# Modulation vectors by transposition and a sum on VectorE, and the last four norms in halves of 256 tokens

## The chip, the core and the metric

One core of one Trainium2 chip runs the whole program in one launch. The metric is the device time of one execution in microseconds (us). Engines in the rows: PE is TensorE (PEld its weight loads), DVE is VectorE, ACT is ScalarE, POOL is GpSimd, SP is SyncE, which only issues transfers.

## What is computed

Two blocks over 512 tokens of 1024 features, float32, one after the other. The first (differential attention, a short convolution, an output product, a gate) is not touched except that four modulation vectors are made beside it. The second, cut to what matters:

```python
def rmsnorm(x, g):
    y = xf * lax.rsqrt(jnp.mean(xf * xf, axis=-1, keepdims=True) + EPS)
    return y * g
def modulate(h, shift, scale):
    return h * (1.0 + scale[:, None, :]) + shift[:, None, :]
...
c_act = jax.nn.silu(c)
for i in range(2):
    mod = c_act @ w_ada[i] + b_ada[i]
    sh1, sc1, g1, sh2, sc2, g2 = jnp.split(mod, 6, axis=-1)
    h = modulate(rmsnorm(x, norm_mix_g[i]), sh1, sc1)
    m = fourier_mixer(h, w_fourier_out) if i == 0 else retention_mixer(h, w_ret_in, w_ret_out)
    x = x + g1[:, None, :] * m
    h = modulate(rmsnorm(x, norm_ffn_g[i]), sh2, sc2)
    x = x + g2[:, None, :] * swiglu(h, w_ffn_in[i], w_ffn_out[i])
shf, scf = jnp.split(c_act @ w_ada_final + b_ada_final, 2, axis=-1)
return modulate(rmsnorm(x, final_norm_g), shf, scf)
```

So there are 14 modulation vectors of 1024 numbers, each a vector times a 1024x1024 matrix, and each norm needs, for every token, the sum of squares over all 1024 features before any feature of it can be scaled.

## The kernel before

Tensors lie feature-major: `X[:, m, :]` is feature tile m (128 features on the partitions) by 512 tokens, m from 0 to 7. A product of K input tiles gives output tile m by K steps (k, m), and each step is three matmuls of 128x128 weights by 512 tokens, since every float32 operand is split in a high and a low part of type float32r: low weights by high data (L1361), high by low (L1364), high by high (L1365). `gemm_order` takes output tiles 0 to 3 together with k outermost (the last two k tile by tile), and then tiles 4 to 7 one after the other. Outputs lie in seven PSUM banks by the tables `BANK` and `TURN`; bank 7 is `aux`, for small products.

Weights come as one stream of 259 chunks of eight 128x128 tiles. SP loads a chunk into a ring of four (L295), ACT writes the high part (`split_w`, L379), POOL the low part in four pieces (L355), and PE signals `w_used` when it begins the next chunk. Every engine's order is written out by hand, and engines wait for each other on semaphores; a wait holds everything behind it on that engine.

**Modulation vectors.** SP streams each 1024x1024 matrix in eight row blocks of 512 KB (L301), and DVE adds them, scaled by `cact`, into `ada_acc` (128x1024; L767 for the first, L770 for the rest). `ada_reduce` on PE then sums over the 128 partitions: eight matmuls with `ada_acc` as the weights and a column of ones as data (L1447), each of which the profile shows as two records. `ada_out` on DVE adds the bias from `aux` (L782). This happens 14 times: once for each of the four heads of the attention, once beside the ple product, seven times in the first feed-forward, twice in the second.

**Norms.** Norms are numbered: v = 4 (`ffn0`, behind the product `fout`), 5 (`rnorm`, behind `down0b`), 6 (`ffn1`, behind `retout`), 7 (`final`, behind `down1b`). Behind each finished output tile DVE updates X (L832) and multiplies by the gain (`gained`, L795), ACT squares (L386), DVE adds the squares (L791). Behind the last tile PE sums over partitions (`norm_stats`: L1436, L1438, then L1429, whose result nobody reads), ACT takes the logarithm and the exponential (L392, L394), DVE multiplies (L813), ACT adds the shift and makes the high part (L405), DVE the low part (L804), for m = 0 to 7. The next product begins with the high part of tile 0 alone (L1387, L1390, eight matmuls), then its low part (L1397, four), then the ordinary steps. Behind the last norm there is no product: DVE scales (L1336), ACT adds the shift (L743), SP stores each tile (L345).

The rows name things by these tiles: `scr` holds the gained X and other scratch, `rinv` the inverse root mean square, `tmp` the product of the two, `a_hi`/`a_lo` the split input of the next product, `b_hi`/`b_lo` that of the products behind the mixer and in `down`, `cols` constants with the identity matrix among them.

## Time and profile before

| | |
|---|---|
| time before, median of 3 | 1616.94 us (1614.03 to 1619.04) |
| the profiled execution, its own time | 1617.48 us |
| its span | 1615.7 us |
| PE, PEld busy | 1572.4, 1286.6 us |
| DVE, ACT, POOL busy | 761.3, 600.3, 879.1 us |
| PE: idle before L1436, before L1387 | 15.4, 8.2 us |
| ada matmuls on PE (L1447), 224 records | 25.9 us |

A timeline row gives the start, the length, engine, line, operation, out<-in (data, then weights), a count, and in brackets the idle time of the engine before it and what ended that. Matmul lengths overlap, so what a matmul costs PE is the distance from its start to the next start. PEclk is the granted clock as a share of 2.4 GHz.

### The profile page before, as it was taken

Reading aid. Unit: us, or ns where it says so; the run is one execution under the profiler, and the core shown is the slowest. Engines: PE = TensorE matmul, PEld = TensorE weight load, DVE = VectorE, ACT = ScalarE, POOL = GpSimd, SP = SyncE. Lnnn points to the kernel's source line nnn. Section 1 sums busy time; section 2 is a strip of 40 time slices with the busy share of each in tenths; the row PEclk is TensorE's granted clock in tenths of the full one; section 3 lists DMA queues with packets and bytes.
Section 4 is the critical chain, followed back from the end, with each engine's and each line's share of the span. In section 5 each row is a group of like instructions: output and inputs, shape, how many; then the busy total and the mean of one; then the engine's idle time right before and its main releaser. Section 6 shows DMA issues by size and latency. Waiting matters only on the chain.

```text
span 1615.7 us, 20944 instructions
## 1 busy us (share of the span) xinstructions
PE 1572.4 (97%) x7110; PEld 1286.6 (80%) x7110; DVE 761.3 (47%) x1048; ACT 600.3 (37%) x857; POOL 879.1 (54%) x1040
## 2 busy tenths in 40 slices
PE   6999999999999999999999999999998999999997
PEld 4778778888788888888778888888876888888885
DVE  6666766687734432542463624435257343111113
ACT  5444434674432211222344434334345322222323
...
GB/s 196 117 183 192 129 116 234 88 127 169 79 157 195 178 193 194 169 201 92 104 78 68 101 93 66 113 65 90 104 52 66 164 187 144 103 94 94 101 78 52
DMA packets 56935, 202.95 MB, mean 126 GB/s; under 512 B 6320, under 2 KB 6320, under 8 KB 56880
## 3 DMA queue, kind: packets, MB, share of 16 engines
...
## 4 chain that ended last, share of the span: by engine, by line
PE 73%; issue 12%; POOL 11%; ACT 1%; DVE 1%; POOLq 0%; DVEq 0%; ACTq 0%
PE banks L1361 21%; PE banks L1365 21%; PE banks L1364 21%; POOL w_lo L355 11%; PE banks L1732 2%; PE banks L1733 2%; PE banks L1729 2%; PE banks L1447 1%; PE banks L1768 1%; PE banks L1769 1%; PE banks L1767 1%; PE banks L1755 0%; PE banks L1756 0%; PE banks L1754 0%; DVE X L832 0%
## 5 line engine op out<-in xcount | busy, mean ns | idle before, releaser
L355 POOL TENSOR_TENSOR w_lo<-w_raw,w_hi 128x256 fp32r<-128x256 f32 x1036 | 878.9, 881 | 706.3 <-ACT w_hi L379 706.1
L379 ACT ACTIVATE w_hi<-w_raw 128x1024 fp32r<-128x1024 f32 x259 | 273.1, 1059 | 668.3 <-PE banks L1361 609.3
L1361 PE MATMUL banks<-a_hi,w_lo 128*128 128x512 f32 x1264 | 499.8, 395 | 0.0
L1365 PE MATMUL banks<-a_hi,w_hi 128*128 128x512 f32 x1264 | 492.7, 390 | 0.0
L1364 PE MATMUL banks<-a_lo,w_hi 128*128 128x512 f32 x1264 | 492.6, 390 | 0.0
L1361 PEld LDWEIGHTS banks<-a_hi,w_lo 128*128 128x128 f32 x1264 | 237.9, 188 | 50.5 <-issue 1.9
L1364 PEld LDWEIGHTS banks<-a_lo,w_hi 128*128 128x128 f32 x1264 | 238.0, 188 | 50.2 <-issue 1.9
L1365 PEld LDWEIGHTS banks<-a_hi,w_hi 128*128 128x128 f32 x1264 | 237.7, 188 | 50.2
L1361 PE MATMUL banks<-b_hi,w_lo 128*128 128x512 f32 x624 | 244.2, 391 | 1.8 <-DVE b_lo L1297 1.7
L1365 PE MATMUL banks<-b_hi,w_hi 128*128 128x512 f32 x624 | 242.9, 389 | 0.0
L1364 PE MATMUL banks<-b_lo,w_hi 128*128 128x512 f32 x624 | 242.8, 389 | 0.0
L770 DVE SCALAR_TENSOR_TENSOR ada_acc<-ada_raw,small,ada_acc 128x1024 f32<-128x1024 f32 x98 | 153.0, 1561 | 64.7 <-DMA ada_raw<-in_ADA 61.9
L1361 PEld LDWEIGHTS banks<-b_hi,w_lo 128*128 128x128 f32 x624 | 117.1, 188 | 27.0 <-DVE b_lo L1297 2.1
L1364 PEld LDWEIGHTS banks<-b_lo,w_hi 128*128 128x128 f32 x624 | 117.2, 188 | 24.6 <-issue 0.5
L1365 PEld LDWEIGHTS banks<-b_hi,w_hi 128*128 128x128 f32 x624 | 117.1, 188 | 24.4
L832 DVE SCALAR_TENSOR_TENSOR X<-banks,mod,X 128x512 f32<-128x512 f32 x72 | 52.9, 747 | 171.5 <-PE banks L1365 171.3
L1138 DVE TENSOR_TENSOR scr<-scr,banks 128x512 f32<-128x512 f32 x44 | 30.3, 688 | 106.3 <-PE banks L1365 105.8
L1134 DVE SCALAR_TENSOR_TENSOR scr<-scr,banks 128x512 f32<-128x512 f32 x44 | 30.3, 689 | 105.8 <-ACT scr L615 105.8
L1146 DVE SCALAR_TENSOR_TENSOR b_lo<-scr,b_hi 128x512 f32 (+1 forms) x44 | 33.3, 757 | 51.3 <-ACT b_hi L622 51.3
L1729 PE MATMUL banks<-w_lo,a_hi 128*128 128x512 f32 x128 | 49.8, 389 | 0.0
L1732 PE MATMUL banks<-w_hi,a_lo 128*128 128x512 f32 x128 | 49.8, 389 | 0.0
L1733 PE MATMUL banks<-w_hi,a_hi 128*128 128x512 f32 x128 | 49.8, 389 | 0.0
...
## 6 DMA issues: line engine op xcount, KB each, us to landing
w_raw<-in_W SPq DMA_DIRECT2D x259, 512.0 KB, 3.4
...
```

What stands on the lines that cost most here:

```text
L355: pool.tensor_tensor(w_lo[:, c % RING, part], w_raw[:, c % RING, part], w_hi[:, c % RING, part].bitcast(fp32), ALU.subtract).then_inc(wlo, 1)
L379: act.activation(w_hi[:, c % RING, :], w_raw[:, c % RING, :], ACT.Copy).then_inc(whi, 1)
L770: ins = dve.scalar_tensor_tensor(out=ada_acc[:, :], in0=src, scalar=cact[:, f:f + 1], in1=ada_acc[:, :], op0=ALU.mult, op1=ALU.add)
L832: read_out(dve.scalar_tensor_tensor(out=X[:, m, :], in0=banks[:, BANK[t], :], scalar=mod[:, KD * g + m:KD * g + m + 1], in1=X[:, m, :], op ...
L1134: read_out(dve.scalar_tensor_tensor(out=SG[:, n, :], in0=T2[:, n, :], scalar=1.0, in1=banks[:, BANK[g], :], op0=ALU.add, op1=ALU.mult), g)
L1146: dve.scalar_tensor_tensor(out=lo, in0=HD[:, n, :], scalar=0.5, in1=hi.bitcast(fp32), op0=ALU.mult, op1=ALU.subtract).then_inc(hid_ready, 1)
L1361: mm = pe.matmul(out, lo, x_hi, start=first, stop=False)
L1364: pe.matmul(out, hi, x_lo, start=False, stop=False)
L1365: mm = pe.matmul(out, hi, x_hi, start=False, stop=last)
L1729: mm = pe.matmul(out, a_hi[:, k, c], wl, start=(k == 0), stop=False)
L1732: pe.matmul(out, a_lo[:, k, c], wh, start=False, stop=False)
L1733: mm = pe.matmul(out, a_hi[:, k, c], wh, start=False, stop=(k == KD - 1))
```

## The change

**Modulation vectors.** In 13 of the 14 places `ada_reduce` becomes `ada_turn`: PE transposes the eight 128x128 pieces of `ada_acc` (identity as data) into two banks (bank 4, in the feed-forwards bank 6, and bank 7), and DVE sums each over its 128 columns (one `tensor_reduce` over 1024 columns, in the heads two over 512) and adds the bias. The place beside ple stays, as `ada_columns`. A hook in the `out` product waits, behind its 32nd step, until the last head's sum has been read.

**Norms 4 to 7.** The last output tile (for v = 6 the last two) is computed as tokens 0 to 255 (FRONT), then tokens 256 to 511 (BACK) with the same weights. X, squares, sum and logarithm of FRONT run beside the matmuls of BACK; the FRONT statistics are a matmul put between BACK's (after 5 of its steps; for v = 6 after 7 of 8). The next product takes its first four k for output tiles 0 to 3 in two passes, FRONT and then BACK, and the statistics of BACK stand between them, behind step (1, 1) of FRONT. Weight tiles of these steps are kept in the ring for both passes, and the `w_used` signals move to the second pass. The unread L1429 and L1791 go in these norms. Two chunk splits on ACT move behind the last squares. The stores become 16 of half the size.

```diff
+HT = S // 2
+KH = 4
+SPLIT = {4: (7,), 5: (7,), 6: (6, 7), 7: (7,)}
+SPLIT_AT = {4: 0, 5: 1, 6: 2, 7: 4}
...
-            for m in range(KD):
-                sp.wait_ge(x_done, m + 1)
-                sp.dma_start(OUT[:, m, :], X[:, m, :]).then_inc(out_done, 16)
-            sp.wait_ge(out_done, 16 * KD)
+            for h, part in ((half_done, FRONT), (x_done, BACK)):
+                for m in range(KD):
+                    sp.wait_ge(h, m + 1)
+                    sp.dma_start(OUT[:, m, part], X[:, m, part]).then_inc(out_done, 16)
+            sp.wait_ge(out_done, 2 * 16 * KD)
...
+            def split_squares(v, t0):
+                act.preload_act_table_set("natural_log_exp_and_others")
+                for n, m in enumerate(SPLIT[v]):
+                    act.wait_ge(half_read, SPLIT_AT[v] + n + 1)
+                    act.wait_ge(sq_added, added(v) + m - 2)
+                    act.activation(sq[:, m % 2, FRONT], X[:, m, FRONT], ACT.Square).then_inc(half_sq, 1)
+            def back_squares(v, t0):
+                for m in SPLIT[v]:
+                    wait_read(act, flat, t0 + m)
+                    act.activation(sq[:, m % 2, BACK], X[:, m, BACK], ACT.Square).then_inc(sq_ready, 1)
+            def front_rsqrt(v):
+                act.wait_ge(half_stats, v - 3)
+                act.activation(rinv[:, FRONT], aux[:, FRONT], ACT.Ln, bias=eps6, scale=1.0 / D).then_inc(half_ln, 1)
+                act.wait_ge(half_ln, v - 3)
+                act.activation(rinv[:, FRONT], rinv[:, FRONT], ACT.Exp, scale=-0.5).then_inc(half_r, 1)
+            def back_rsqrt(u):
+                act.wait_ge(aux_ready, u + 1)
+                act.activation(rinv[:, BACK], aux[:, BACK], ACT.Ln, bias=eps6, scale=1.0 / D).then_inc(aux_free, 1)
+                act.wait_ge(aux_free, u + 1)
+                act.activation(rinv[:, BACK], rinv[:, BACK], ACT.Exp, scale=-0.5).then_inc(r_ready, 1)
+            def split_norm(v, a, u, t0, shift, c):
+                def hi(m, part):
+                    act.activation(a_hi[:, m, part], tmp[:, m % 2, part], ACT.Identity,
+                                   bias=shift(m)).then_inc(half_hi if part is FRONT else h_hi, 1)
+                def front(m):
+                    act.wait_ge(half_h, KH * (a - 1) + m + 1)
+                    hi(m, FRONT)
+                split_squares(v, t0)
+                front_rsqrt(v)
+                front(0)
+                front(1)
+                back_squares(v, t0)
+                split_w(flat, c + 2)
+                front(2)
+                front(3)
+                back_rsqrt(u)
+                for m in range(KD):
+                    if m == KH:
+                        split_w(flat, c + 3)
+                    act.wait_ge(h_ready, 8 * a + m + 1)
+                    hi(m, BACK if m < KH else slice(0, S))
...
+                if bank is None:
+                    dve.tensor_tensor(dst, aux[:, 0:KD], b, ALU.add).then_inc(aux_free, 1)
+                    return
+                if bank == 6:
+                    turned = banks[:, 6:8, :].rearrange("p a (f q) -> p (a f) q", q=P)
+                    link(dve.tensor_reduce(ada_col, turned, AX.X, ALU.add), at)
+                else:
+                    for n, half in enumerate((bank, 7)):
+                        turned = banks[:, half, :].rearrange("p (f q) -> p f q", q=P)
+                        ins = dve.tensor_reduce(ada_col[:, 4 * n:4 * n + 4], turned, AX.X, ALU.add)
+                    link(ins, at)
+                dve.tensor_tensor(dst, ada_col, b, ALU.add).then_inc(aux_free, 1)
...
+                last = SPLIT[v]
+                dve.wait_ge(half_r, v - 3)
+                dve.wait_ge(xg_s, 8 * (a + 1) - len(last))
+                mult(0, FRONT)
+                mult(1, FRONT)
+                for m in last:
+                    split_tile(v, t0, m, g, BACK, True)
+                lo(0, FRONT)
+                for m in last:
+                    split_add(v, m, BACK, True)
+                lo(1, FRONT)
+                mult(2, FRONT)
+                mult(3, FRONT)
+                lo(2, FRONT)
+                lo(3, FRONT)
+                for m in last:
+                    wait_read(dve, flat, t0 + m)
+                    gained(name, m, gained_by)
+                dve.wait_ge(r_ready, NORMS[name] + 1)
+                dve.wait_ge(xg_s, 8 * (a + 1))
+                for m in range(KD):
+                    mult(m, BACK if m < KH else slice(0, S))
+                    if m:
+                        lo(m - 1, BACK if m - 1 < KH else slice(0, S))
+                lo(KD - 1, slice(0, S))
...
+            residuals(t0, range(KD - 2), 8, 6, "ffn1", 4, True)
+            add_square(6, KD - 3)
+            front_end(6, t0, 8)
...
+            t0 = TI["down1b"]
+            dve.wait_ge(half_r, 4)
+            scaled(0, FRONT, half_scaled)
+            scaled(1, FRONT, half_scaled)
+            split_tile(7, t0, KD - 1, 11, BACK, True)
+            scaled(2, FRONT, half_scaled)
+            split_add(7, KD - 1, BACK, True)
+            for m in range(3, KD):
+                scaled(m, FRONT, half_scaled)
             dve.wait_ge(r_ready, 8)
             for m in range(KD):
-                dve.scalar_tensor_tensor(out=X[:, m, :], in0=X[:, m, :], scalar=gs[:, m:m + 1], in1=rinv[:, :],
-                                         op0=ALU.mult, op1=ALU.mult).then_inc(x_scaled, 1)
+                scaled(m, BACK, x_scaled)
...
+            def part_mul(out, weights, x, part, first, last, signals=None):
+                (_, hi, lo), (x_hi, x_lo) = weights, x
+                mm = pe.matmul(out, lo, x_hi[:, part], start=first, stop=False)
+                if signals is not None:
+                    mm.then_inc(signals, 1)
+                pe.matmul(out, hi, x_lo[:, part], start=False, stop=False)
+                return pe.matmul(out, hi, x_hi[:, part], start=False, stop=last)
+            def split_tiles(v, t0, ks, rhs, ready, mid):
+                kept = {}
+                pe.wait_ge(aux_free, AUX[("ffn0", "rnorm", "ffn1", "final")[v - 4]])
+                if v in (4, 6):
+                    wait_read(pe, flat, t0 + 1)
+                for m in SPLIT[v]:
+                    out = front_of(v, m)
+                    for n, k in enumerate(ks):
+                        ready(k)
+                        kept[m, k] = chunk_begins(flat, P)
+                        signals = w_used if kept[m, k][0] and not kept_before(kept, m, k) else None
+                        mm = part_mul(out, kept[m, k], rhs(k), FRONT, n == 0, n == len(ks) - 1, signals)
+                mm.then_inc(half_ready, 1)
+                count = 0
+                for m in SPLIT[v]:
+                    out = banks[:, BANK[t0 + m], BACK]
+                    wait_bank(flat, t0 + m)
+                    for n, k in enumerate(ks):
+                        signals = w_used if kept[m, k][0] and kept_before(kept, m, k) else None
+                        mm = part_mul(out, kept[m, k], rhs(k), BACK, n == 0, n == len(ks) - 1, signals)
+                        count += 1
+                        if count == mid:
+                            pe.wait_ge(half_sum, SPLIT_AT[v] + len(SPLIT[v]))
+                            pe.matmul(aux[:, FRONT], ones[:, :], sqsum[:, FRONT], start=True,
+                                      stop=True).then_inc(half_stats, 1)
+                    mm.then_inc(tile_ready, 1)
...
+            def back_stats(v):
+                pe.wait_ge(full_sum, v - 3)
+                pe.wait_ge(half_ln, v - 3)
+                pe.matmul(aux[:, BACK], ones[:, :], sqsum[:, BACK], start=True, stop=True).then_inc(aux_ready, 1)
+            def split_start(t0, a, v, rhs):
+                tiles = {}
+                for part in (FRONT, BACK):
+                    his, los = (half_hi, half_a) if part is FRONT else (h_hi, a_ready)
+                    base = KH * (a - 1) if part is FRONT else KD * a
+                    for k in range(KH):
+                        x = rhs(k)
+                        x_hi, x_lo = x
+                        for m in range(4):
+                            if part is FRONT:
+                                if k == 0:
+                                    wait_bank(flat, t0 + m)
+                                tiles[k, m] = chunk_begins(flat, P)
+                        if k == 0:
+                            pe.wait_ge(his, base + 1)
+                            for m in range(4):
+                                begins, hi, lo = tiles[k, m]
+                                out = banks[:, BANK[t0 + m], part]
+                                mm = pe.matmul(out, lo, x_hi[:, part], start=part is FRONT, stop=False)
+                                if begins and part is FRONT:
+                                    mm.then_inc(w_used, 1)
+                                pe.matmul(out, hi, x_hi[:, part], start=False, stop=False)
+                            pe.wait_ge(los, base + 1)
+                            for m in range(4):
+                                out = banks[:, BANK[t0 + m], part]
+                                pe.matmul(out, tiles[k, m][1], x_lo[:, part], start=False, stop=False)
+                            continue
+                        pe.wait_ge(los, base + k + 1)
+                        for m in range(4):
+                            signals = w_used if tiles[k, m][0] and part is BACK else None
+                            part_mul(banks[:, BANK[t0 + m], part], tiles[k, m], x, part, False, False, signals)
+                            if part is FRONT and (k, m) == (1, 1):
+                                back_stats(v)
...
+            def ada_turn(at, u, g, bank):
+                pe.wait_ge(ada_sum, at("ada", KD * (g + 1)))
+                pe.wait_ge(aux_free, at("aux", u))
+                for f in range(KD):
+                    out = banks[:, bank if f < KD // 2 else 7, f % 4 * P:(f % 4 + 1) * P]
+                    mm = pe.transpose(out, ada_acc[:, f * P:(f + 1) * P], ident)
...
-            gemm(flat, TI["fout"], KD, range(KD), rhs_b, lambda k: pe.wait_ge(f_ready, k + 1))
-            norm_stats(4, "ffn0")
+            gemm(flat, TI["fout"], KD, range(KD), rhs_b, lambda k: pe.wait_ge(f_ready, k + 1), split=4, mid=5)
```

How the order moves, at three places. On PE in the first `with_ada` loop of the first feed-forward, before:

```order
L1364 MATMUL banks<-a_lo,w_hi 128x512
L1365 MATMUL banks<-a_hi,w_hi 128x512
L1444 ISA
L1445 REGISTER_ALU
L1447 MATMUL banks<-ones,ada_acc 128x1 x8
L1361 MATMUL banks<-a_hi,w_lo 128x512
```

The eight products stand between two ordinary steps. At the same place of PE's order now:

```order
L1562 MATMUL banks<-a_lo,w_hi 128x512
L1563 MATMUL banks<-a_hi,w_hi 128x512
L1740 ISA
L1741 REGISTER_ALU
L1744 MATMUL banks<-cols,ada_acc 128x128 x8
L1559 MATMUL banks<-a_hi,w_lo 128x512
```

Eight one-column products have become eight transposes at the same place.

On PE from the last matmuls of `fout` into the first feed-forward, before (`b_hi`: input of `fout`; `a_hi`: input of the feed-forward):

```order
L1365 MATMUL banks<-b_hi,w_hi 128x512
L1436 MATMUL banks<-sqsum,ones 128x512
L1438 MATMUL banks<-sq,ones 128x512
L1429 MATMUL banks<-cols,ones 128x512
L1387 MATMUL banks<-a_hi,w_lo 128x512
L1390 MATMUL banks<-a_hi,w_hi 128x512
```

The statistics follow the last matmul of `fout`. At the same place of PE's order now:

```order
L1579 MATMUL banks<-b_hi,w_hi 128x256
L1605 MATMUL banks<-sqsum,ones 128x256
L1575 MATMUL banks<-b_hi,w_lo 128x256
L1578 MATMUL banks<-b_lo,w_hi 128x256
L1579 MATMUL banks<-b_hi,w_hi 128x256
L1575 MATMUL banks<-b_hi,w_lo 128x256
L1578 MATMUL banks<-b_lo,w_hi 128x256
L1579 MATMUL banks<-b_hi,w_hi 128x256
L1575 MATMUL banks<-b_hi,w_lo 128x256
L1578 MATMUL banks<-b_lo,w_hi 128x256
L1579 MATMUL banks<-b_hi,w_hi 128x256
L1637 MATMUL banks<-a_hi,w_lo 128x256
```

The first statistics now stand nine matmuls ahead of the end of `fout`, at half the width, and the second have gone behind the first steps of the next product.

On DVE at the same place, before, from the last tile's X on:

```order
L832 SCALAR_TENSOR_TENSOR X<-banks,mod,X 128x512
L795 TENSOR_SCALAR scr<-X,gs 128x512
L813 TENSOR_TENSOR tmp<-scr,rinv 128x512 x2
L804 SCALAR_TENSOR_TENSOR a_lo<-tmp,mod,a_hi 128x512
L813 TENSOR_TENSOR tmp<-scr,rinv 128x512
```

Everything is 512 tokens wide. From the same tile on, DVE's order now:

```order
L923 SCALAR_TENSOR_TENSOR X<-banks,mod,X 128x256
L944 TENSOR_TENSOR sqsum<-sqsum,sq 128x256
L962 TENSOR_TENSOR tmp<-scr,rinv 128x256 x2
L923 SCALAR_TENSOR_TENSOR X<-banks,mod,X 128x256
L968 SCALAR_TENSOR_TENSOR a_lo<-tmp,mod,a_hi 128x256
L944 TENSOR_TENSOR sqsum<-sqsum,sq 128x256
L968 SCALAR_TENSOR_TENSOR a_lo<-tmp,mod,a_hi 128x256
L962 TENSOR_TENSOR tmp<-scr,rinv 128x256 x2
L968 SCALAR_TENSOR_TENSOR a_lo<-tmp,mod,a_hi 128x256 x2
L891 TENSOR_SCALAR scr<-X,gs 128x512
```

BACK's X and squares now stand between the scaled tiles of FRONT, and the gained tile 7 stands behind them.

## Rows read from the trace of the kernel before

**Rows 1.** The page: span, and busy time by engine.

```profile
span 1615.7 us, 20944 instructions
...
PE 1572.4 (97%) x7110; PEld 1286.6 (80%) x7110; DVE 761.3 (47%) x1048; ACT 600.3 (37%) x857; POOL 879.1 (54%) x1040
```

**Rows 2.** Timeline of PE at the first modulation sum, first head.

```profile
88.45 1.90 PE L1447 MATMUL banks<-ones,ada_acc 128*128 128x1 f32 x16
...
90.53 0.39 PE L1364 MATMUL banks<-a_lo,w_hi 128*128 128x512 f32 x1
```

**Rows 3.** Timeline of PE at four transposes of softmax weights, first head.

```profile
74.27 0.60 PE L1479 MATMUL banks<-cols,scr 128*128 128x128 f32 x4
...
74.94 0.39 PE L1364 MATMUL banks<-a_lo,w_hi 128*128 128x512 f32 x1
```

**Rows 4.** Timelines of DVE and of PE in the second head.

```profile
95.15 1.84 DVE L770 SCALAR_TENSOR_TENSOR ada_acc<-ada_raw,small,ada_acc 128x1024 f32<-128x1024 f32 x1 [1.47 <-DMA ada_raw<-in_ADA]
...
102.75 1.49 DVE L770 SCALAR_TENSOR_TENSOR ada_acc<-ada_raw,small,ada_acc 128x1024 f32<-128x1024 f32 x1 [4.43 <-DMA ada_raw<-in_ADA]
...
105.77 0.69 DVE L931 SCALAR_TENSOR_TENSOR scr<-tmp,banks 128x512 f32<-128x512 f32 x1 [0.50 <-ACT tmp L455]
...
118.83 1.22 DVE L893 TENSOR_REDUCE small<-scr 128x2 f32<-128x1024 f32 x1
...
110.59 0.33 PE L1479 MATMUL banks<-cols,scr 128*128 128x128 f32 x1 [0.36 <-DVE b_lo L935]
```

**Rows 5.** Timeline of all engines at norm ffn0.

```profile
423.71 0.39 PE L1365 MATMUL banks<-b_hi,w_hi 128*128 128x512 f32 x1
...
424.14 0.75 DVE L832 SCALAR_TENSOR_TENSOR X<-banks,mod,X 128x512 f32<-128x512 f32 x1 [2.73 <-PE banks L1365]
...
426.87 0.69 ACT L392 ACTIVATE rinv<-banks,small 128x512 f32<-128x512 f32 x1
...
429.75 0.50 PE L1387 MATMUL banks<-a_hi,w_lo 128*128 128x512 f32 x1 [2.16 <-ACT a_hi L405]
...
434.20 0.39 PE L1361 MATMUL banks<-a_hi,w_lo 128*128 128x512 f32 x1
```

**Rows 6.** Timelines of DVE and of PE at norm ffn1.

```profile
1226.68 0.75 DVE L832 SCALAR_TENSOR_TENSOR X<-banks,mod,X 128x512 f32<-128x512 f32 x1
...
1229.84 0.39 PE L1365 MATMUL banks<-b_hi,w_hi 128*128 128x512 f32 x1
...
1243.16 0.40 PE L1361 MATMUL banks<-a_hi,w_lo 128*128 128x512 f32 x1
```

**Rows 7.** Timelines from the last product to the end, and of SP at the start.

```profile
1602.53 1.02 PE L1436 MATMUL banks<-sqsum,ones 128*128 128x512 f32 x2
...
1607.70 5.36 ACT L743 ACTIVATE X<-X,mod 128x512 f32<-128x512 f32 x8 [0.89 <-DVE X L1336]
1608.45 4.97 SPq L345 DMA_DIRECT2D out<-X  x8
...
0.75 3.95 SPq L304 DMA_DIRECT2D X<-in_XT  x8
```

**Rows 8.** Timeline of PE in the first Fourier product: matmuls 256 columns wide.

```profile
353.05 0.28 PE L1609 MATMUL banks<-w_hi,b_lo 128*128 128x256 f32 x1
353.17 0.28 PE L1610 MATMUL banks<-w_hi,b_hi 128*128 128x256 f32 x1
```

**Rows 9.** Groups of one shape: DVE and ACT at half width (count, busy us, mean ns).

```profile
L905 DVE SCALAR_TENSOR_TENSOR scr<-scr,small 128x256 f32<-128x256 f32 x4 | 1.9, 484 | 0.1
...
L596 ACT ACTIVATE scr<-banks 128x258 f32<-128x258 f32 x4 | 1.5, 370 | 2.3 <-PE banks L1639 2.3
```

**Rows 10.** One window: busy by engine, then PEclk; and PE's timeline behind a wait.

```profile
362.00:364.00 2.00, 2.00 (x12) 2.00 (x12) 0.56 (x2) 2.00 (x5) 1.43 (x3) 0.56 0.00 0
...
1208.17 0.50 PE L1361 MATMUL banks<-b_hi,w_lo 128*128 128x512 f32 x1 [1.69 <-DVE b_lo L1297]
...
1215.79 0.39 PE L1361 MATMUL banks<-b_hi,w_lo 128*128 128x512 f32 x1
```

195 lines of the change are left out of this document (142 added, 53 removed).

## Prediction

> **What bounds the kernel now.** I read the page's busy times first, then PE's timeline at its waits, at the sums and at the norms. PE is busy 1572.4 of 1615.7 us [rows 1]. Behind a wait at 1208 its ordinary matmuls of 512 columns go on without a gap, 33 of them in 7.62 us [rows 10]; the first is slow to start, and I take 0.227 for each. So nearly every microsecond of PE is on the path, and time can be won in three places: what PE does beside the ordinary steps, its waits at the norms, and the tail behind its last product. Work added to DVE (47% busy) or ACT (37%) costs only where PE or the tail waits for it.
>
> **Modulation sums, on PE.** From the first of a sum's sixteen records to the second ordinary matmul behind them are 90.53 - 88.45 = 2.08 us [rows 2]; less one ordinary distance, one sum costs PE 1.85 us. In the same way four transposes cost 74.94 - 74.27 - 0.23 = 0.44 us [rows 3], 0.11 each; eight cost 0.9. A sum gets cheaper by 0.95 us, and thirteen change: at most 12.4 us.
>
> A transpose that reads `ada_acc` is not in the trace; its shape and type are those of rows 3, so I take their price. The bound on the other side is the length of one, 0.27 (0.60 us for four, of which three distances of 0.11 are overlap): if they did not overlap, eight would cost 2.2 us and each sum 0.3 more than now. The Trainium skill speaks for this bound: "TensorE: Matmul & The Clock Gate", section "Part 4: PE-mode transpose", gives about 275 ns for a transpose in a kernel. By it, were they one behind the other, the thirteen would lose some 4.5 us instead of winning 12. Rows 3 speak against it.
>
> **Modulation sums, on DVE.** A reduction of 1024 columns out of PSUM is not in the trace; the nearest is one of 1024 out of SBUF, 1.22 us [rows 4]. Two halves and a link make about 1.6 us in the heads, against some 0.2 for the bias alone. Bounds 1.0 and 2.0. In the feed-forwards nobody waits for it: DVE stood waiting for the sum itself, and the bank that PE needs next is some 20 steps away. In the heads the queue behind it on DVE is the next head's bias, L767, L770 and the first softmax. L770 stood 1.47 us for its transfer [rows 4], which takes the added 1.4; the next one stood 4.43.
>
> But in heads 2 to 4 PE already waits, 0.36 us in the second, for DVE's `b_lo` at the transposes of the first weights [rows 4]. That chain comes from the transfer that lands at 102.75, through the softmax, not from PE; if PE comes 0.95 earlier it waits longer. The one piece that can move is the 0.50 for which L931 stood behind ACT's tanh [rows 4], and the tanh waits for PE. So three of the four head sums give 0.5 each (bounds 0 and 0.95). The fourth, with no head behind it, and the nine in the feed-forwards give all: 10 x 0.95 + 3 x 0.5 = **11.0 us** (9.5 to 12.4).
>
> **Half widths.** A matmul of 256 columns starts 0.12 behind the one before [rows 8] (0.119 over a longer row of them); two cost 0.238 against 0.227. On DVE an operation on two tensors of 256 columns takes 0.48 [rows 9] where L832 takes 0.75 for 512 [rows 5]; ACT takes 0.37 for 258 out of PSUM [rows 9]. So a half saves about 0.27 on DVE and 0.21 on ACT: X 0.48, adds and products 0.42, square 0.42, Ln 0.48, Exp 0.42, shift 0.51.
>
> **Norm ffn0.** Let zero be the end of tile 6. Tile 7 is 24 matmuls, 5.45 us, and ends at 423.94; the first ordinary step behind the norm starts at 434.20 [rows 5], that is at 15.7, with 12 matmuls of the next product done. 48 are done 36 x 0.227 later, at 23.9.
> Now FRONT of tile 7 lasts to 2.86. DVE starts 0.2 behind a tile's end (424.14 [rows 5]): X to 3.5, square to 4.0, add to 4.4. PE has done 15 matmuls of BACK at 4.64 and does not wait; the statistics, a full float32 matmul of 256 columns, take 0.43. BACK ends at 6.14. From X to Ln were 2.73 us before [rows 5]: less 0.75, 0.63 and 0.86 for X, square and statistics, the handoffs are 0.5, of which I put 0.4 ahead of Ln. So Ln starts at 5.5, Exp ends at 6.4, DVE's product at 6.85, ACT's shift at 7.4, and PE begins at 7.44: **a wait of 1.3**, where it had 2.16 [rows 5] behind one of 0.65. DVE has BACK's X, the low part of tile 0 (8.1) and BACK's add ahead of the low part of tile 1 (9.0), for which PE waits 0.2 more. From there PE has work: 36 halves, 0.43 of statistics, 48 halves, to 19.5. Beside it, one behind the other, ACT splits a chunk and makes the second Ln and Exp (to 11.6), DVE the gained tile 7; the first BACK tile is ready at 13.8, just as PE gets there. Gain 23.9 - 19.5 = **4.4**.
>
> **Norm rnorm** goes like ffn0 before, but tile 7 has ten steps, so 15 matmuls of BACK follow the statistics, not 9. By the same steps PE waits 0.6 and 0.2. Gain **5.0**.
>
> **Norm ffn1.** The last matmul of `retout` starts at 1229.84 [rows 6], so tile 5 ended 1224.6, my zero. The matmul that starts at 1243.16 [rows 6] has 15 of the next product ahead of it; 48 are done at 26.0. DVE is late here: X of tile 5 stood at 1226.68 [rows 6], 2.1 behind. With the gained tile and two adds it comes to FRONT of tiles 6 and 7 at 4.5, and their sum is ready at 6.3; PE stands there from 5.36, a wait of 0.9. Ln, Exp, product and shift take until 9.1, BACK ended at 7.1: wait 2.0. The two X and two adds of BACK cost 0.8 more. 48 are done at 21.9: gain 4.1 at full clock.
>
> **The clock.** Before, the first twelve matmuls behind ffn0 took 434.20 - 429.75 = 4.45 us [rows 5] instead of 2.72: 1.7 lost, most of them at 1.2 GHz, the lower level. All three norms paid it, and it is in their times above. Will it be paid again? A wait of 1.69 at 1208 was followed by matmuls at full pace [rows 10]; 2.16 behind 0.65 was not. So ffn0 (1.3) and rnorm (0.6) probably keep the clock and ffn1 (0.9, then 2.0) does not: minus 1.7. The three norms give 4.4 + 5.0 + 2.4 = **11.8** (5 to 14).
>
> **The tail.** Tile 6 of the last product ended thirty matmuls ahead of 1602.53 [rows 7], 20.0 us ahead of the span's end. Now rinv of FRONT is ready at 7.1 behind it, the scaling of FRONT runs under and behind BACK, and the second Exp ends at 11.6. ACT has 16 operations of 0.44 (eight full ones took 5.36 [rows 7]), and ends at 16.2, where it ended at 17.3. But SP issues no faster than one transfer in 0.52 (eight in 3.95, the last one's own 0.33 taken off [rows 7]): the eight BACK stores, from 13.4 on, are issued by 17.1 and the last lands at 19.5. Gain **0.5** (-0.5 to 1.5).
>
> **Sum.** 11.0 + 11.8 + 0.5 = 23.3 us. Against the profiled execution's own 1617.5 that is 1594.2; the median of the runs is 0.5 lower, so about 1594.
>
> **Rivals.** Everything covered: the clock stays up at ffn1 too, and the heads give all four sums, 3 us more, **1591**. For it, DVE has spare time in the heads; against it, PE's wait there.
>
> The handoffs eat the norms. POOL's splits fall on DVE's small operations and stretch them, each norm waits 1 us more (3.0), PE loses its clock at ffn0 and rnorm too (3.4), and the heads give nothing (1.5 of mine): with the tail's lower bound (1.0) **1603**. For it: a norm is a chain of six handoffs, and halving shortens none.
>
> The ring starves the halves: two chunks are held for both passes, PE waits for a chunk in the steps behind, and only the sums remain, **1606**. Against it: the fifth chunk's slot comes free at 16.6 and is needed at 30.
>
> The transposes do not overlap (bound above): the 11.0 go and 4.2 are added, **1609**.
>
> Slower than before: narrow matmuls bring the clock down for as long as they last. In one window of [rows 10] PE is all busy with 258 columns and PEclk is 0.56. The change makes 252 matmuls into 504 halves (24 + 30 + 24 + 30 at the ends of products, 3 x 48 at their starts). At 1.2 GHz one needs 0.213 for its columns, 0.094 more: 47 us, **1640**. It turns the sign from 250 halves at the lower level on. Against it: nine microseconds earlier the same width ran at 0.12 [rows 8], which only the upper level allows.
>
> **How the numbers follow.** Forecast 1594: 50%. Everything covered 15%, handoffs 22%, ring 5%, transposes 3%, narrow clock 5%. 1587 to 1605 takes in the first three with the bounds of the heads (1.5), of the norms and the median's own spread (2.5): 87%. Less than 0.3% (4.9 us) cannot be told from no change. Faster 0.92, same 0.03 (the transposes' case, with its spread), slower 0.05.
>
> **What would show it.** In the profile after: groups of eight transposes of `ada_acc`, 1.1 us long; PE's wait for `b_lo` in the heads grown to 0.8; reductions near 1.2 us; PE's wait for `a_hi` 1.3, 0.6 and 2.0 at the three norms; PEclk at 1.0 behind ffn0 and rnorm and lower behind ffn1; SP, not ACT, setting the pace of the last stores. I am wrong if PE waits elsewhere: for weights in the steps behind a norm, or for the half sum ahead of the first statistics.

## The result and the profile after

| | before | after |
|---|---|---|
| median of the runs | 1615.84 us (1614.03 to 1619.04, 4 runs) | 1596.89 us (1595.53 to 1598.29, 4 runs) |
| the profiled execution, its own time | 1617.48 us | 1598.29 us |
| its span | 1615.7 us | 1596.5 us |

The ratio is 0.9881, 95% interval [0.9861, 0.99]. In a second session the changed kernel had 1594.9 us (1592.75 to 1601.86, 5 runs), ratio 0.985 [0.9833, 0.9866]. The forecast was 1594, from 23.3 us won; the two spans differ by 19.2.

The page of after, to be laid beside [rows 1]: PE has 18.2 us less, DVE 34 more.

```profile
span 1596.5 us, 21361 instructions
...
PE 1554.2 (97%) x7250; PEld 1284.7 (80%) x7250; DVE 795.3 (50%) x1111; ACT 606.1 (38%) x890; POOL 883.6 (55%) x1040
```

What PE waited for, from the view of waits of after (who waited, for what: us in all, times, longest). L1776 is the heads; L1559 for `w_lo` is new and stands in the `out` product; L1637 and L1605 are the three norms that have a product behind them; L1616 is the statistics of BACK in the last norm, in the tail.

```profile
PE banks L1776 <- DVE b_lo L1115: 7.2, 4, 2.8
PE banks L1637 <- ACT a_hi L463: 3.4, 3, 1.8
PE banks L1559 <- POOL w_lo L374: 1.9, 1, 1.9
...
PE banks L1616 <- DVE sqsum L944: 1.5, 1, 1.5
...
PE banks L1605 <- DVE sqsum L944: 1.1, 1, 1.1
```

To find where the 19.2 us came from I read on PE's timeline the starts of the modulation sums and of the norms' statistics, which both kernels have, and took the distances between them.

| stage of PE | before | after | won | forecast |
|---|---|---|---|---|
| start to the first head's sum | 88.45 | 88.69 | -0.24 | 0 |
| three heads, sum to sum | 162.00 | 162.81 | -0.81 | 2.45 with the next row |
| fourth sum to the statistics behind `out` | 37.88 | 39.16 | -1.28 | |
| from there to the first feed-forward's first sum (norm ffn0) | 173.77 | 169.65 | 4.1 | 4.4 |
| from there to the seventh sum | 272.20 | 266.49 | 5.7 | 5.7 |
| to the first sum of the second feed-forward (seventh sum, rnorm, ffn1) | 579.62 | 570.94 | 8.7 | 8.4 |
| from there to the end (two sums, tail) | 301.8 | 298.8 | 3.0 | 2.4 |

Everything behind `out` came out 0.6 us better than forecast. The heads and `out` (the first three rows) were to win 2.45 us and lost 2.33: that is the whole miss.

**Sums.** The first sum on PE in after, to be laid beside [rows 2]:

```profile
88.69 1.04 PE L1744 MATMUL banks<-cols,ada_acc 128*128 128x128 f32 x8
89.49 0.47 PE L1559 MATMUL banks<-a_hi,w_lo 128*128 128x512 f32 x1
89.80 0.39 PE L1562 MATMUL banks<-a_lo,w_hi 128*128 128x512 f32 x1
```

Eight transposes cost 89.80 - 88.69 - 0.23 = 0.88 us, as forecast. In the feed-forwards the distance from sum to sum fell from 45.37 to 44.41.

**Norms.** PE at ffn0, rnorm and ffn1 (statistics of FRONT, first matmul of the next product, statistics of BACK):

```profile
425.50 0.59 PE L1605 MATMUL banks<-sqsum,ones 128*128 128x256 f32 x2
...
428.50 0.35 PE L1637 MATMUL banks<-a_hi,w_lo 128*128 128x256 f32 x1 [1.34 <-ACT a_hi L463]
...
430.72 0.59 PE L1616 MATMUL banks<-sqsum,ones 128*128 128x256 f32 x2
...
796.30 0.35 PE L1637 MATMUL banks<-a_hi,w_lo 128*128 128x256 f32 x1 [0.32 <-ACT a_hi L463]
...
1218.09 0.70 PE L1605 MATMUL banks<-sqsum,ones 128*128 128x256 f32 x2 [1.06 <-DVE sqsum L944]
...
1220.90 0.55 PE L1637 MATMUL banks<-a_hi,w_lo 128*128 128x256 f32 x1 [1.75 <-ACT a_hi L463]
```

Waits forecast 1.3, 0.6, and 0.9 with 2.0: measured 1.34, 0.32, and 1.06 with 1.75. The clock went as forecast too: two windows of after (busy us of PE, PEld, DVE, ACT and POOL with counts, PEclk, then DMA share and GB/s), behind ffn0 at the upper level, behind ffn1 at the lower.

```profile
430.00:432.00 2.00, 2.00 (x17) 1.94 (x16) 2.00 (x3) 1.60 (x4) 2.00 (x3) 1.00 0.00 0
...
1222.00:1224.00 2.00, 2.00 (x11) 2.00 (x11) 1.90 (x5) 0.84 (x2) 1.19 (x2) 0.50 0.00 0
```

**The tail.** ACT's last eleven pieces and SP's sixteen stores:

```profile
1588.93 4.48 ACT L817 ACTIVATE X<-X,mod 128x256 f32<-128x256 f32 x11
...
1585.74 8.94 SPq L364 DMA_DIRECT2D out<-X  x16
```

The first stores still wait for ACT (the sixth for 0.8 us). From 1589.85 on SP issues without a pause, ten stores 0.49 us apart:

```profile
1589.85 4.84 SPq L364 DMA_DIRECT2D out<-X  x10
```

ACT makes a piece every 0.40 us there, and SP is done at 1594.69, 1.3 us behind ACT's end: SP sets the pace of the last stores.

### The profile page after: what moved, and what is told of

The parts are those of the page before. It is cut to its first block, busy times and chain, and to the rows that moved or that the text cites. A ratio compares the mean times of both kernels' runs of the same rounds, so it can differ in the third digit from the quotient of the medians.

```text
span 1596.5 us, 21361 instructions
## 1 busy us (share of the span) xinstructions
PE 1554.2 (97%) x7250; PEld 1284.7 (80%) x7250; DVE 795.3 (50%) x1111; ACT 606.1 (38%) x890; POOL 883.6 (55%) x1040
## 4 chain that ended last, share of the span: by engine, by line
PE 81%; issue 9%; POOL 8%; DVE 1%; ACT 1%; POOLq 0%; ACTq 0%; DVEq 0%
PE banks L1559 22%; PE banks L1563 22%; PE banks L1562 22%; POOL w_lo L374 8%; PE banks L2030 2%; PE banks L2034 2%; PE banks L2033 2%; PE banks L1575 1%; PE banks L2070 1%; PE banks L2068 1%; PE banks L2069 1%; PE banks L1578 1%; PE banks L1579 1%; PE banks L1744 0%; PE banks L2055 0%
## 5 line engine op out<-in xcount | busy, mean ns | idle before, releaser
L1559 PE MATMUL banks<-a_hi,w_lo 128*128 128x512 f32 x1228 | 485.9, 396 | 0.0
L1563 PE MATMUL banks<-a_hi,w_hi 128*128 128x512 f32 x1228 | 479.2, 390 | 0.0
L1562 PE MATMUL banks<-a_lo,w_hi 128*128 128x512 f32 x1228 | 479.0, 390 | 0.0
L1559 PEld LDWEIGHTS banks<-a_hi,w_lo 128*128 128x128 f32 x1228 | 231.3, 188 | 49.0 <-issue 2.2
L1559 PE MATMUL banks<-b_hi,w_lo 128*128 128x512 f32 x588 | 230.2, 392 | 3.6 <-POOL w_lo L374 1.9
L1563 PE MATMUL banks<-b_hi,w_hi 128*128 128x512 f32 x588 | 228.9, 389 | 0.0
L1562 PE MATMUL banks<-b_lo,w_hi 128*128 128x512 f32 x588 | 228.8, 389 | 0.0
L855 DVE SCALAR_TENSOR_TENSOR ada_acc<-ada_raw,small,ada_acc 128x1024 f32<-128x1024 f32 x98 | 152.5, 1556 | 66.9 <-DMA ada_raw<-in_ADA 64.2
L1559 PEld LDWEIGHTS banks<-b_hi,w_lo 128*128 128x128 f32 x588 | 110.4, 188 | 27.6 <-issue 3.0
L1563 PEld LDWEIGHTS banks<-b_hi,w_hi 128*128 128x128 f32 x588 | 110.4, 188 | 23.2
L1562 PEld LDWEIGHTS banks<-b_lo,w_hi 128*128 128x128 f32 x588 | 110.4, 188 | 23.1 <-issue 0.5
```

The source lines that it names most:

```text
L855: ins = dve.scalar_tensor_tensor(out=ada_acc[:, :], in0=src, scalar=cact[:, f:f + 1], in1=ada_acc[:, :], op0=ALU.mult, op1=ALU.add)
L1559: mm = pe.matmul(out, lo, x_hi, start=first, stop=False)
L1562: pe.matmul(out, hi, x_lo, start=False, stop=False)
L1563: mm = pe.matmul(out, hi, x_hi, start=False, stop=last)
```

## Where the heads' gain went

In the second head the step that was to absorb DVE's new work did absorb it. DVE in after, to be laid beside [rows 4]: the reductions are there (1.28 us), the step behind them no longer waits for its transfer, and L1111 no longer waits for ACT.

```profile
92.19 1.28 DVE L876 TENSOR_REDUCE small<-banks 128x4 f32<-128x512 f32 x2
...
95.03 1.01 DVE L852 TENSOR_SCALAR ada_acc<-ada_raw,small 128x1024 f32<-128x1024 f32 x1
96.07 1.63 DVE L855 SCALAR_TENSOR_TENSOR ada_acc<-ada_raw,small,ada_acc 128x1024 f32<-128x1024 f32 x1
...
103.32 1.62 DVE L855 SCALAR_TENSOR_TENSOR ada_acc<-ada_raw,small,ada_acc 128x1024 f32<-128x1024 f32 x1 [4.29 <-DMA ada_raw<-in_ADA]
...
106.31 0.67 DVE L1111 SCALAR_TENSOR_TENSOR scr<-tmp,banks 128x512 f32<-128x512 f32 x1
...
110.21 0.69 DVE L1115 TENSOR_TENSOR b_lo<-banks,b_hi 128x512 fp32r<-128x512 f32 x1 [1.64 <-ACT b_hi L530]
```

But the step that waits for the next transfer began at 103.32 instead of 102.75, and `b_lo` began at 110.21 instead of 109.84. The prediction had this landing fixed and `b_lo` 0.5 us earlier. PE, 0.9 earlier with its sum, waited for it:

```profile
110.96 0.33 PE L1776 MATMUL banks<-cols,scr 128*128 128x128 f32 x1 [1.42 <-DVE b_lo L1115]
```

Why was it later? DVE's first step, POOL and SP in before, then POOL and SP in after (POOL: pieces of chunk splits; SP: issue of a chunk and of a modulation block):

```profile
92.93 0.75 DVE L767 TENSOR_SCALAR ada_acc<-ada_raw,small 128x1024 f32<-128x1024 f32 x1
...
93.78 9.37 POOL L355 TENSOR_TENSOR w_lo<-w_raw,w_hi 128x256 fp32r<-128x256 f32 x12 [3.77 <-ACT w_hi L379]
...
97.76 0.33 SPq L295 DMA_DIRECT2D w_raw<-in_W  x1
98.28 0.44 SPq L301 DMA_DIRECT2D ada_raw<-in_ADA  x1
```

```profile
93.86 10.00 POOL L374 TENSOR_TENSOR w_lo<-w_raw,w_hi 128x256 fp32r<-128x256 f32 x12 [3.77 <-ACT w_hi L398]
...
98.48 0.33 SPq L313 DMA_DIRECT2D w_raw<-in_W  x1
99.00 0.33 SPq L319 DMA_DIRECT2D ada_raw<-in_ADA  x1
```

The block's slot is free when L852 ends (96.04), but SP issues it at 99.00, behind a chunk, and that chunk waits until POOL has split an older one. From POOL's start to the chunk's issue it was 3.98 us before and is 4.62 now. What moved is DVE's first step: before, L767 ended ahead of the split, and only L770 ran beside it (its fourth piece took 1.71 us, the first three 0.74 each). Now L1104 and L852 run beside the second and third pieces (0.93 and 1.17 us), and L855 beside the fourth (1.72, as before). My theory for the experiments: **the pace of a head is set by the chain POOL's split, chunk, block behind it in SP's queue, DVE's third step, softmax, `b_lo`; PE's saving falls into its wait.** The rivals: DVE's longer work alone sets the pace, or the loss is made elsewhere.

## Where the loss in `out` comes from

Behind the heads ACT loads PT, waits for it, copies it, and has three chunk splits queued behind. ACT and PE in after:

```profile
253.80 0.34 ACTq L560 DMA_DIRECT2D scr<-in_PT  x1
...
259.50 1.06 ACT L562 ACTIVATE b_hi<-scr 128x1024 fp32r<-128x1024 f32 x1 [5.21 <-DMA scr<-in_PT]
260.46 2.94 ACT L398 ACTIVATE w_hi<-w_raw 128x1024 fp32r<-128x1024 f32 x3
...
266.05 0.47 PE L1559 MATMUL banks<-b_hi,w_lo 128*128 128x512 f32 x1 [1.93 <-POOL w_lo L374]
```

SP issued a chunk at 253.14 and a modulation block at 253.67; the three transfers are in flight together, and PT lands after 5.7 us. Before, PT was issued at 252.12, 0.47 ahead of SP's pair, and landed after 3.6.

## The experiments

Each was timed in several executions beside the kernel before, whose median was 1617.0 us beside heads_columns, norms_only, sums_only and step_late, 1617.4 beside pt_behind, sp_ada_first, step_late_pt and before_step_late, and 1617.2 beside the rest; that of the first session of after stands above. The stages, from each one's trace:

| kernel | start to first sum | three heads | `out` | PE's waits for `b_lo`, heads 1 to 4 | median us | ratio to before |
|---|---|---|---|---|---|---|
| before | 88.45 | 162.00 | 37.88 | 2.34, 0.36, 0.35, 0.45 | | 1 |
| after | 88.69 | 162.81 | 39.16 | 2.84, 1.42, 1.41, 1.56 | 1596.9 | 0.9881 |
| after_again | 89.11 | 162.77 | 42.40 | 2.34, 1.40, 1.38, 1.52 | 1594.9 | 0.985 |
| heads_columns | 87.86 | 162.23 | 37.89 | 2.34, 0.33, 0.33, 0.42 | 1596.6 | 0.9875 |
| norms_only | 87.91 | 163.03 | 41.19 | 2.34, 0.33, 0.33, 0.42 | 1605.7 | 0.993 |
| sums_only | 89.23 | 161.65 | 36.93 | 2.34, 1.24, 0.60, 1.58 | 1605.6 | 0.9928 |
| step_late | 84.11 | 159.36 | 39.88 | 1.51, 0.33, 0.33, 0.42 | 1591.5 | 0.9839 |
| late_columns | 84.22 | 161.94 | 39.08 | 1.52, 0.33, 0.33, 0.42 | 1594.4 | 0.9855 |
| sp_ada_first | 84.77 | 161.32 | 38.16 | 1.79, 0.51, 0.52, 0.44 | 1593.0 | 0.9858 |
| reduce_twice | 88.75 | 160.69 | 36.93 | 2.83, 1.42, 0.35, 0.66 | 1593.7 | 0.9855 |
| pt_behind | 87.47 | 162.29 | 36.92 | 2.34, 1.25, 1.39, 1.48 | 1594.9 | 0.9866 |
| step_late_pt | 85.11 | 159.90 | 36.93 | 0.95, 0.34, 0.33, 0.42 | 1589.5 | 0.9834 |
| all_three | 84.64 | 161.56 | 37.00 | 1.56, 0.33, 0.33, 0.42 | 1591.1 | 0.9833 |
| before_step_late | 85.09 | 162.00 | 39.21 | 0.92, 0.35, 0.35, 0.44 | 1611.8 | 0.9965 |

The intervals of the ratios reach 0.0013 to 0.0020 to either side, some 2 to 3 us. So medians 3 us apart are weak evidence, and the stages of the traces carry the argument where they agree.

**The parts apart.** `norms_only` makes all sums as before; `sums_only` is the kernel before with the thirteen transposed sums (its diff is the sums' part of the one shown ahead).

```diff
-                    ada_turn(at, A0 + 6, 0, 4)
+                    ada_columns(at, A0 + 6, 0)
...
-                            ada_turn(at, u + more, g + more, 6)
+                            ada_columns(at, u + more, g + more)
```

> Only the second half of the change: the last four norms in halves, all fourteen sums as one-column products. The traces give 4.2 us at ffn0, 4.7 at rnorm, 3.0 at ffn1 and 1.1 at the tail, 13.0 together: 1603 us. Rival: the parts are not independent (the norms' gain needs what the sums leave), then it is above 1605.

> Only the first half of the change: thirteen sums by transposition, norms whole. Theory: nine sums in the feed-forwards give 0.95 each (8.6 us), the four in the heads give nothing, and the heads and the out product lose 2.3 us: 6.3 us won, 1609.5. Rival: the loss in the heads and in out comes from elsewhere in the change, then 11.0 us are won, 1604.8.

The parts alone win 11.3 and 11.4 us (1617.03 less 1605.7 and 1605.59). In `norms_only` the stage of ffn0 took 169.67, as in after. Its median is 2.7 above my 1603; its trace lost 0.9 at the fourth sum, for which PE waited, and 3.3 in `out`, where PE then ran at the lower clock until 259. The sums won 5 more than the stages of after had promised, and came out at the rival's 11.0. In the trace of `sums_only` (1608.4 us, its slowest execution) one of the three heads took 53.3 and `out` lost nothing; why the other executions won still more stays open. The parts are additive within the intervals (0.993 x 0.9928 = 0.9859), and the loss in the heads and `out` is not of a fixed size.

**The head sums undone.** `heads_columns` is the changed kernel with the first pair of the diff above alone.

> The changed kernel (1596.9 us), but the four head sums are made as before (one-column products, bias alone on DVE); the nine in the feed-forwards stay transposed. Theory: in the heads PE's saving of 0.95 us is lost again in its wait for b_lo, because a chain through DVE sets the pace of a head, and DVE's added 1.3 us lengthens it; before the change a head took 53.98 us, now 54.27, and the out product has a new wait of 1.93 us. Undoing it makes the kernel 1 to 2.5 us faster (1594.4 to 1596), PE's wait in the second head falls from 1.42 to about 0.36. Rival, the working of the prediction: each head sum is worth 0.5 to 0.95, so undoing four costs 2.5 us: 1599.4.

Measured 1596.6, between what the theory and the rival gave (after has 1596.9 and 1594.9). PE's wait in the second head fell to 0.33, as the theory has it, and a head takes what it took with the transposes: 54.1 against 54.3. In the changed kernel the four transposed head sums are worth nothing; they do no clear harm either, and the 1 to 2.5 us that the theory promised for undoing them are not in the medians.

**The step that stands for the transfer, moved.** `step_late`:

```diff
                 softmax_a(at, 0)
-                ada(at, 1)
                 softmax_b(at, 0)
...
                 softmax_a(at, 1)
+                ada(at, 1)
```

> The changed kernel, but the third step of the modulation sum in a head stands on DVE behind the second block's first softmax part, not ahead of the first block's second part. There DVE stood 4.42 us for that step's transfer, with the first softmax queued behind it. Theory: the landing of this transfer sets the pace of a head, through the softmax to b_lo for which PE waits 1.4 us in each of heads 2 to 4 and 2.8 in the first: PE's wait falls under 0.4, 3 to 5 us are won, 1592 to 1594. Rival: DVE's own added work (1.3 us of reductions) sets the pace, the transfer is only what it stands at: no change, 1597.

1591.5 us, and a head takes 53.1: the 0.95 of the sum is now won in each. PE at the same place as above has its 0.33 again:

```profile
105.29 0.33 PE L1776 MATMUL banks<-cols,scr 128*128 128x128 f32 x1 [0.33 <-DVE b_lo L1115]
```

The first head won most, 4.6 us with the start. Two windows there, after and then `step_late`: behind a wait of 2.84 the clock is at its lower level, behind 1.51 it stays up.

```profile
56.00:58.00 2.00, 2.00 (x6) 1.61 (x5) 1.63 (x4) 1.09 (x3) 1.95 (x3) 0.50 0.00 0
```

```profile
54.00:56.00 2.00, 2.00 (x10) 1.64 (x9) 1.65 (x4) 0.99 (x3) 2.00 (x3) 1.00 0.86 346
```

In the trace of `step_late` one stage lost time. At ffn0 PE stood for the half sum ahead of the first statistics, where it had not stood in after, and the stage from `out` to the first sum took 171.39 us, 1.7 more than in after:

```profile
419.83 0.70 PE L1605 MATMUL banks<-sqsum,ones 128*128 128x256 f32 x2 [1.45 <-DVE sqsum L944]
```

DVE was late there: three of its adds (L887) in the 7 us ahead of FRONT's X took 1.23, 1.22 and 1.04 us beside pieces of POOL's splits, where one without a piece beside it takes 0.69. In after such adds stood further ahead, and DVE had time to wait for PE again. So it reads in the trace; no run tested it, and no other trace with the halves shows this wait at ffn0.

Is it the transfer, or would any order of this kind win? Two controls. `late_columns` has the moved step and the head sums as before; `before_step_late` is the kernel before with the moved step alone.

> The sum's third step late on DVE (as in step_late, 1591.5 us), and the four head sums as one-column products on PE (as in heads_columns). Theory: with the transfer out of the chain a head is bound by PE, so each head sum is now worth its 0.95 us on PE: a head takes 54.0 instead of 53.1, and the kernel 1595.3, 3.8 us above step_late. Rival: a head sum costs or gives nothing wherever the step stands: 1591.5.

> The kernel before, with only the sum's third step moved late on DVE. Theory: PE waited there 2.3 us in the first head and 0.36 in the others, so at most 3.4 us can be won, about 1 to 3: 1613 to 1615. Rival: the same 3 to 5 us as in the changed kernel, which would say that the step's place costs the same with and without the transposed sums.

`late_columns`: a head takes 53.9 to 54.1, every one with a wait of 0.33 to 0.42, so PE sets the pace and a sum is worth its full price there; 1594.4 us, 3.0 above `step_late` where 3.8 were expected. `before_step_late`: heads of 53.9 to 54.1 as without the move, so in the kernel before the transfer cost nothing beyond the first head. That one won 3.4, the most that I had allowed: its wait is 1.4 shorter, and behind it (0.92) the clock stays up. The kernel won more than forecast, 5.6 us (1611.8 against 1617.4), and so the rival's number, but not in the heads: in the traces `out` lost 1.3, and 3.1 came from the stages of ffn0 and rnorm, where the clock stayed up this time and which the move does not touch.

**The queue's order.** `sp_ada_first`: SP issues the block ahead of the chunk of the same step.

```diff
-                load_w(at, pos[0], at.i is None and pos[0] < RING)
-                pos[0] += 1
                 for _ in range(k):
                     load_ada(at, pos[1], at.i is None and pos[1] < ADA_RING)
                     pos[1] += 1
+                load_w(at, pos[0], at.i is None and pos[0] < RING)
+                pos[0] += 1
```

> The changed kernel, but SP issues a modulation block ahead of the weight chunk of the same step, not behind it. Theory: the block for which DVE stands 4.42 us was issued at 153.17 because the chunk ahead of it in SP's queue waited until 152.64 for POOL to finish a split, while its own slot was free at 151.9: it is issued 1.2 us earlier, PE's waits in the heads shrink by about 1 us each, 1593 to 1594. Rival: the two transfers then overlap as before and land together: no change. Other side: chunks are issued later in the rest of the kernel, PE or ACT waits for weights: above 1598.

SP and DVE in the second head: the block goes 0.18 us behind the end of L852, and DVE waits 1.39 for it, not 4.29.

```profile
92.47 0.33 SPq L319 DMA_DIRECT2D ada_raw<-in_ADA  x1
94.74 0.33 SPq L313 DMA_DIRECT2D w_raw<-in_W  x1
```

```profile
91.29 1.00 DVE L852 TENSOR_SCALAR ada_acc<-ada_raw,small 128x1024 f32<-128x1024 f32 x1
92.33 1.63 DVE L855 SCALAR_TENSOR_TENSOR ada_acc<-ada_raw,small,ada_acc 128x1024 f32<-128x1024 f32 x1
96.67 1.76 DVE L855 SCALAR_TENSOR_TENSOR ada_acc<-ada_raw,small,ada_acc 128x1024 f32<-128x1024 f32 x1 [1.39 <-DMA ada_raw<-in_ADA]
```

1593.0 us, as the theory had it, though it had the slot freed a step too late: what the block loses behind the chunk is 3 us, not 1.2. The heads do not win all (161.32, not 159.4): in two of them PE now waits 0.57 and 0.41 for `ada_acc` at the sum itself.

**DVE's work, doubled.** `reduce_twice` makes the reductions in the heads twice, the first time into columns that nobody reads.

```diff
-                    for n, half in enumerate((bank, 7)):
+                    for n, half in ((2, bank), (3, 7), (0, bank), (1, 7)):
```

> The changed kernel with DVE's reductions in the heads made twice (the first result is not used), 1.28 us more of DVE in each head. Theory: DVE stands 4.4 us later on for a transfer, which was issued behind a weight chunk and not when DVE freed its slot; the added work goes into that idle time, a head grows by 0.5 at most, 1597 to 1599. Rival: DVE's own work sets the pace of a head, each grows by 1.3: 1602.

This is the sharpest of them. With 1.2 us more work on DVE in each head the kernel is not slower (1593.7 against 1594.9 of after in the same session), and the third and fourth heads are faster by a microsecond (53.0 and 53.4 against 54.2 and 54.5). So DVE's length is not what sets the pace. DVE, POOL and SP in the fourth head, in after (POOL's rows overlap: the piece of 205.04 is the second of the row above it, and lasts until 203.91 + 2.86 = 206.77) and then in `reduce_twice`:

```profile
204.53 1.63 DVE L855 SCALAR_TENSOR_TENSOR ada_acc<-ada_raw,small,ada_acc 128x1024 f32<-128x1024 f32 x1
212.20 1.28 DVE L855 SCALAR_TENSOR_TENSOR ada_acc<-ada_raw,small,ada_acc 128x1024 f32<-128x1024 f32 x1 [4.71 <-DMA ada_raw<-in_ADA]
...
203.91 2.86 POOL L374 TENSOR_TENSOR w_lo<-w_raw,w_hi 128x256 fp32r<-128x256 f32 x2
...
205.04 2.42 POOL L374 TENSOR_TENSOR w_lo<-w_raw,w_hi 128x256 fp32r<-128x256 f32 x2
...
206.94 0.33 SPq L313 DMA_DIRECT2D w_raw<-in_W  x1
```

```profile
199.59 2.48 DVE L876 TENSOR_REDUCE small<-banks 128x4 f32<-128x512 f32 x4
...
209.18 1.76 DVE L855 SCALAR_TENSOR_TENSOR ada_acc<-ada_raw,small,ada_acc 128x1024 f32<-128x1024 f32 x1 [1.38 <-DMA ada_raw<-in_ADA]
...
201.26 2.12 POOL L374 TENSOR_TENSOR w_lo<-w_raw,w_hi 128x256 fp32r<-128x256 f32 x3 [3.77 <-ACT w_hi L398]
...
204.42 0.33 SPq L313 DMA_DIRECT2D w_raw<-in_W  x1
```

In after the split began at 202.33, and its fourth piece, from 205.04 to 206.77 beside DVE's L855, took 1.73 us; the chunk went right behind it, 4.61 us behind the split's start. In `reduce_twice` the first three pieces, beside the reductions and the small steps behind them, took 2.12 together, and the chunk went 3.16 us behind the start. So the split is short where DVE reads PSUM beside it and long where DVE streams SBUF. More work on DVE moved L855 behind the split, the chunk went 1.45 us sooner after the split's start, and DVE's wait for the block behind it shrank from 4.71 to 1.38 (the added 1.2 us of work fills part of it). In the second head the chunk went as early (3.17), but the block took 5.5 us to land instead of 4.2 as in the fourth, and there nothing was won (54.3). That POOL is stretched by DVE's SBUF work is read from these durations; no kernel changed it alone. The Trainium skill ("SBUF — State Buffer", section "SBUF: two separate sides") says that VectorE, with two inputs in SBUF, and GpSimd take a shared port pair in turn, each for a whole instruction; the 1.73 us agree with that, and so does DVE's own loss (1.63 us instead of 1.28), since a piece of POOL's was under way when its step began.

**`out`.** `pt_behind`: ACT splits three chunks before it waits for PT (DVE's low part moves likewise).

```diff
-            act.wait_ge(p_in, 16)
-            act.activation(b_hi[:, 8:10, :].rearrange("p k s -> p (k s)"), PV, ACT.Copy).then_inc(p_hi, 1)
             c0, t0 = CH["out"], TI["out"]
             for n in range(8):
                 if n != 3:
                     split_w(flat, c0 + n + 4)
+                if n == 2:
+                    act.wait_ge(p_in, 16)
+                    act.activation(b_hi[:, 8:10, :].rearrange("p k s -> p (k s)"), PV, ACT.Copy).then_inc(p_hi, 1)
```

> The changed kernel, but in the out product ACT splits three chunks before it waits for the transfer of PT, and DVE makes its low part behind two steps of the sum. Theory: the new wait of 1.93 us for w_lo at 266.05 comes from the splits queued on ACT behind a transfer that shares the DMA engines with another one issued 0.13 us before it (5.7 us to landing, 3.6 before the change): the wait goes, 1595.0. Rival: POOL's splits are late for another reason, the wait stays: 1597.

The wait is gone, though PT took 5.6 us to land in this trace too; `out` takes 36.92 us, which is the 37.88 of before less the sum's 0.95. One trace without the wait would say little: of the eleven traces without this move, `before` among them, five have no such wait either. In them PT was issued ahead of SP's pair, or over 1 us behind it, and landed within 4.6 us; in the six with the wait it took 4.8 to 7.3. The three traces with the move have PT landing after 4.8 to 5.6 us and no wait. And the changed kernel as it is, once more:

> The changed kernel as it is, in one call with the others, to see how far its head stage and its wait in out come out the same in another execution: 1596.9 as before. If the 1.93 us wait for w_lo is a matter of which transfers meet in one execution, it is absent or of another size here; if it is fixed, it is 1.9.

It is of another size: the wait is there again, longer, and so is the time that ACT stood for PT:

```profile
261.52 1.06 ACT L562 ACTIVATE b_hi<-scr 128x1024 fp32r<-128x1024 f32 x1 [6.83 <-DMA scr<-in_PT]
...
268.07 0.47 PE L1559 MATMUL banks<-b_hi,w_lo 128*128 128x512 f32 x1 [3.58 <-POOL w_lo L374]
```

`out` took 42.40 us here, 5.5 more than in `pt_behind`: behind the wait of 3.58 the clock was at its lower level until about 272. This profiled execution took 1601.86 us, the others of the same kernel 1592.75 to 1596.51, so most of them must have been spared most of it. With the moved wait the runs lie within 1594.37 to 1595.43. `pt_behind` removes a hazard more than it wins time: its median is 2.0 below that of after in one session and equal to it in the other.

**Together.**

> Both moves together: the sum's third step late on DVE and the PT copy behind three splits. Theory: 5 to 7 us won against the changed kernel, 1590 to 1592, faster than either kernel. Rival: one of the two hides the other (if heads are faster, PT no longer shares the DMA engines): 1592 to 1594.

> The three moves together: the sum's third step late on DVE, PT's copy behind three splits, SP's modulation blocks ahead of the chunks. Theory: the first and the third take away the same wait in the heads, so nothing is added to step_late_pt (1589.5), 1588.5 to 1590.5. Rival: SP's order wins something of its own outside the heads (it was 1 us ahead at the second Fourier product): 1587. Other side: chunks issued later make PE wait for w_lo in out or behind it by 1 to 2 us: 1591.

1589.5 us, ratio 0.9834 [0.9821, 0.9848], and 1591.1, 0.9833 [0.9819, 0.9847]: the two moves on DVE and ACT beat the changed kernel by 5 to 7 us, and the queue's order adds nothing to them; its own waits for `ada_acc` (up to 1.14) take its gain.

## Why the prediction was near, and what failed in it

- **The price of a sum on PE** (1.85 to 0.9): right, 0.88 measured. The nine in the feed-forwards gave 0.96 each. The rival without overlap is out.
- **The head sums, 2.45 of the 11.0: the failed step.** "L770 stood 1.47 us for its transfer, which takes the added 1.4; the next one stood 4.43." The first half is right (L855 no longer waits at that place); the second treats the landing of the next transfer as a fixed time. It hangs, through SP's queue, on a split of POOL that was longer by 0.64 with DVE's first step moved beside it. `b_lo` came 0.37 later instead of 0.50 earlier, and PE's wait grew to 1.4, not 0.8. `step_late` shows that this transfer set the pace, `reduce_twice` that DVE's length did not; that DVE's steps stretch the split is read from durations. Of the rival of the handoffs one part, "the heads give nothing", came true, and the heads even lost 1.05.
- **`out`: no term at all.** The sum added nothing for the place behind the last head, where a transfer on ACT's queue came to stand against two of SP's. PE waited 1.93 and 3.58 us there in two traces of the changed kernel, and the stage took 2.2 and 5.5 us more than in `pt_behind`, the second with the clock down; in four others the wait was 0.9 to 2.7, in `before_step_late` too, which has none of the transposed sums. How often in the unprofiled executions stays open.
- **The norms**: ffn0 4.4 forecast, 4.1; rnorm 5.0, 4.7; ffn1 2.4, 3.0. Here the working held to a few tenths. At ffn1 the sum took off two things that do not come together: 1.7 for the clock (it cost 1.4: 3.1 us from the first start to the fifteenth, 1.7 behind ffn0) and 0.8 for waits behind the first matmuls. Those waits are in `late_columns` and `sp_ada_first`, where the clock stayed up (0.47 and 0.58); in after, at the lower clock, PE did not stand there. One of its premises was too strong: "all three norms paid" for the clock. Whole norms with the same two waits of 0.65 and 2.16 did not always pay. `before_step_late` kept the upper clock at both of them and was 1.5 us shorter from the statistics behind `out` to the first sum (172.28 against 173.77), `sums_only` kept it at rnorm alone. The halves kept it at ffn0 and rnorm in every trace of theirs, so part of their gain, up to 1.6 each, is that of a stage that no longer depends on it. At ffn1 it fell in after, as forecast, but stayed up in `late_columns` and `sp_ada_first` behind the same two waits (1.06 and 1.75): there the forecast was partly luck.
- **The tail**: 0.5 forecast, 1.1 measured (254.34 from the last sum to the end, 256.4 before, less the sum's 0.96), inside its bounds. SP set the pace of the last ten stores, as forecast, with 0.49 a store where 0.52 were taken.
- **The narrow matmuls** did not bring the clock down: they ran 0.12 apart behind ffn0 and rnorm, and at ffn1, where they began at the lower level, 0.21 apart, the clock rose to 1.00 while they ran. The rival of the starved ring is out: behind the norms no wait for weights stands. That of the handoffs is out for the norms of after (waits of 1.34, 0.32 and 1.75), but what it feared is seen once: in `step_late` DVE was late from adds beside POOL's splits, and PE stood 1.45 ahead of the first statistics of ffn0.
- The errors added up to 4.8 missing and 0.6 over; the second session's median (1594.9) hides most of it, and that is no merit of the working.
